# RWKV-7 chunk inverse: first products of one direction share a wave with second products of the other

## What is computed

```python
def step(S, inp):
    r_t, w_t, k_t, v_t, kk_t, a_t = inp
    sa = jnp.einsum("bhvk,bhk->bhv", S, -kk_t)
    S = S * w_t[:, :, None, :] + sa[..., None] * (kk_t * a_t)[:, :, None, :] + v_t[..., None] * k_t[:, :, None, :]
    return S, jnp.einsum("bhvk,bhk->bhv", S, r_t)
```

## Time and profile before

| | |
|---|---|
| median of 3 runs | 2392.87 us (2391.01 to 2393.35) |
| profiled execution | 2385.16 us, its span 2383.5 us |
| TensorE busy over the span | 2128.2 us, 89% |
| VectorE busy | 851.2 us, 36% |
| ScalarE busy | 392.8 us, 16% |
| GpSimd busy | 156.5 us, 7% |
| first products L1199 | 1920 records, 218 ns each in the middle |
| second products L1210, L1212 | 1920 and 1536 records, 218 ns |
| the inverse of the first pair starts at | 611.0 us |
| the last second product of the last pair at | 1204.6 us |

### The profile page before, as it was taken

The page is one execution under the profiler, slowest core; times in us unless marked ns, Lnnn a source line. Parts: engine busy times, 40 slices in busy tenths (PEclk is TensorE's granted clock), DMA queues, the critical chain, the costliest instruction groups (busy, mean ns, idle before and its releaser), DMA issues. The chain is left out here.

```text
span 2383.5 us, 38135 instructions
## 1 busy us (share of the span) xinstructions
PE 2128.2 (89%) x16348; PEld 1071.7 (45%) x16348; DVE 851.2 (36%) x1816; ACT 392.8 (16%) x788; POOL 156.5 (7%) x185
## 2 busy tenths in 40 slices
PE   5787799979999999999979979889988998899886
PEld 2244455535666666665655543224322432243222
DVE  1262243434565666666631032112211221122113
ACT  1111112222322332233101010001000100010002
POOL 0000111110110111011101000000000000000000
PEclk9798899999999999999989989999999999999998
DMA  9932899963121211111113199999999999999996
GB/s 365 354 86 84 279 343 354 336 203 82 50 51 41 51 41 49 41 51 39 47 49 97 53 356 413 413 413 413 413 413 413 413 413 413 413 413 413 413 413 269
DMA packets 271136, 594.01 MB, mean 249 GB/s; under 512 B 25869, under 2 KB 166247, under 8 KB 249863
## 3 DMA queue, kind: packets, MB, share of 16 engines
q1 hardware_dynamic: 253575, 524.64, 59.0%
q0 software_dynamic: 17408, 67.11, 7.4%
HBM read 586.89 MB, written 4.82 MB: 248 GB/s over the span
## 5 line engine op out<-in xcount | busy, mean ns | idle before, releaser
L1852 PE MATMUL bank<-arena,picked 128*64 128x512 f32 x1280 | 301.6, 616 | 50.4 <-DMA arena<-exp_w_up 47.7
L1076 PE MATMUL bank<-arena,w_rkv 128*128 128x384 f32 x768 | 283.7, 504 | 12.7 <-DMA w_rkv<-w_in 8.2
L2031 DVE TENSOR_TENSOR x_sum<-x_sum,bank 128x512 f32<-128x512 f32 x180 | 115.4, 684 | 325.6 <-PE bank L1837 325.6
L1852 PEld LDWEIGHTS bank<-arena,picked 128*64 128x64 f32 x1280 | 97.5, 141 | 245.9 <-issue 245.1
L1076 PEld LDWEIGHTS bank<-arena,w_rkv 128*128 128x128 f32 x768 | 136.9, 190 | 102.7 <-issue 18.6
L1852 PE MATMUL bank<-w_exp,picked 128*64 128x512 f32 x768 | 174.9, 597 | 8.5 <-DMA w_exp<-exp_w_up 8.2
L1876 PE MATMUL bank<-w_exp,hid 128*64 128x512 f32 x768 | 176.4, 598 | 6.7 <-DMA w_exp<-exp_w_down 6.7
L690 PE MATMUL bank<-arena,w_xz 128*128 128x384 f32 x448 | 157.3, 500 | 15.0 <-DMA w_xz<-w_in 15.0
L1918 ACT COPY gu<-bank 112x512 f32<-112x512 f32 x32 | 17.2, 589 | 690.0 <-PE bank L1852 690.0
L690 PEld LDWEIGHTS bank<-arena,w_xz 128*128 128x128 f32 x448 | 82.6, 192 | 94.8 <-issue 30.3
L1049 POOL TENSOR_TENSOR WI<-WX,cst 128x384 f32<-128x384 f32 x80 | 80.9, 1027 | 592.1 <-DVE WX L1505 388.4
(11 more groups left out here) (377 smaller groups left out, 2558.1 us busy)
## 6 DMA issues: line engine op xcount, KB each, us to landing
w_exp<-exp_w_down SPq DMA_DIRECT2D x96, 1024.0 KB, 20.9
arena<-exp_w_gate SPq DMA_DIRECT2D x80, 1024.0 KB, 18.9
arena<-exp_w_up SPq DMA_DIRECT2D x80, 1024.0 KB, 19.0
w_ada<-w_ada POOLq DMA_DIRECT2D x64, 1024.0 KB, 8.2
w_exp<-exp_w_gate SPq DMA_DIRECT2D x48, 1024.0 KB, 18.3
w_exp<-exp_w_up SPq DMA_DIRECT2D x48, 1024.0 KB, 18.5
w_ada<-w_ada SPq DMA_DIRECT2D x32, 1024.0 KB, 17.8
arena<-exp_w_down SPq DMA_DIRECT2D x32, 1024.0 KB, 18.2
```

The lines of the kernel that those rows point to most:

```text
L1076: mm = pe.matmul(ps[feed_bank(i)][:, 0:T], w[:, m % 3, n % 8], hT[:, n % KC], start=(n % KC == 0), stop=(n % KC == KC - 1))
L1852: mm = pe.matmul(ps[b][COLS[j], :], picked[:, k, at:at + 64], halves[j][:, c * 1024 + b * 512:c * 1024 + (b + 1) * 512], start=(k == 0), s ...
L2031: V.tensor_tensor(y, y if e else x, ps[(LAST_BANKS[i // 2 % 4] if e == LAST else 6) + i % 2][:], ALU.add).then_inc(S("added"), 1)
```

## The change

TensorE's ten bursts of each pair become eleven waves. `wave(d, n)` holds the first products of direction d of level n and the second products of the other direction o = 1 - d, of level n - 1 if d is 0, of level n if d is 1. It waits for all of its inputs at its head. Wave (0,1) has only first products, wave (0,6) only second ones of direction 1. Inside a chunk the order is: first product of head 0, XT's product, first product of head 1, XT's product, then the two products for X. Behind each wave stand two or three feed matmuls (38 before the inverse's end, as before), `gate(p)` moves from the end of level 2 to behind wave (0,3), and `front` of TensorE moves to behind waves (0,3), (1,3), (0,4) and (1,4). ScalarE's copies keep their order, with the copy of g and some front steps now between them. On VectorE the updates, `end` and the FRONT steps keep their order; only the adds of output chunks move (table ADDS).

```diff
             AHEAD = (2, 4, 8, 11)
-            per_level = ((0, 2, 0, 4), (0, 2, 0, 4), (0, 2, 0, 3), (0, 2, 0, 2), (0, 4, 0, 2))
-            FED = [AHEAD[3] + sum(sum(per_level, ())[:n]) for n in range(21)]
+            FED = 38
...
-                for n in range(1, 6):
-                    for d in range(2):
+                def wave(d, n):
+
+
+                    o, m = 1 - d, n - 1 + d
+                    firsts, seconds = n <= 5, m >= 1
+                    if firsts:
                         pe.wait_ge(S(f"CT_ready{d}"), 5 * p + n)
                         pe.wait_ge(S(f"X_ready{d}"), 5 * p + n)
-                        hold()
-                        for c in range(NCH):
+                    if seconds:
+                        pe.wait_ge(S(f"P1_out{o}"), 5 * p + m)
+                    hold()
+                    for c in range(NCH):
+                        at = slice(c * Q, (c + 1) * Q)
+                        for h in range(2):
+                            here, there = HP[h], HP[1 - h]
+                            if firsts:
+                                m1 = pe.matmul(ps[3 * d][there, at], CT[d][here, c], X[d][here, c], start=True, stop=True)
+                            if seconds and m < 5:
+                                m2 = pe.matmul(ps[3 * o + 2][there, at], P1[o][there, c], XT[o][there, c], start=True, stop=True)
+                        if seconds:
                             for h in range(2):
...
+                                m2 = pe.matmul(ps[3 * o + 1][HP[h], at], XT[o][HP[1 - h], c], P1[o][HP[1 - h], c], start=True, stop=True)
+                    if firsts:
+                        m1.then_inc(S(f"P1_in{d}"), 1)
+                    if seconds:
+                        m2.then_inc(S(f"D_in{o}"), 1)
...
+                for n in range(1, 6):
+                    wave(0, n)
+                    if n == 3:
+                        more_of(2)
+                        gate(p)
+                        more_of(1)
+                    else:
+                        more_of((3, 3, 0, 2, 2)[n - 1])
+                    if n in (3, 4) and more:
+                        front(p + 1, n - 3 + n // 4)
+                    wave(1, n)
+                    more_of((3, 3, 2, 2, 2)[n - 1])
+                    if n in (3, 4) and more:
+                        front(p + 1, 2 * n - 5)
+                wave(0, 6)
+                more_of(FED - fed)
...
+            ADDS = {(1, 0): 1, (2, 1): 2, (4, 1): 3, (5, 1): 4}
...
-                        if d == 1 and n != 3:
-                            add_part(p, (1, 2, None, 3, 4)[n - 1])
+                        if (n, d) in ADDS:
+                            add_part(p, ADDS[(n, d)])
```

More of the change, by code:

```diff
@@ L1191, in body @@
                 feed(p, AHEAD[3] - 1, AHEAD[3])
-                for n in range(1, 6):
-                    for d in range(2):
+                def wave(d, n):
+                    o, m = 1 - d, n - 1 + d
+                    firsts, seconds = n <= 5, m >= 1
+                    if firsts:
                         pe.wait_ge(S(f"CT_ready{d}"), 5 * p + n)
                         pe.wait_ge(S(f"X_ready{d}"), 5 * p + n)
-                        hold()
-                        for c in range(NCH):
-                            for h in range(2):
[L1199 to L1221, removed]
@@ new lines, in wave, with more_of @@
+                    if firsts:
+                        m1.then_inc(S(f"P1_in{d}"), 1)
+                    if seconds:
+                        m2.then_inc(S(f"D_in{o}"), 1)
+                fed = AHEAD[3]
+                def more_of(k):
+                    nonlocal fed
+                    feed(p, fed, fed + k)
+                    fed += k
+                for n in range(1, 6):
[12 more added lines that the diff above has]
+                        front(p + 1, 2 * n - 5)
@@ L1230, in body @@
                 mm.then_inc(S("PU_in"), 1)
-                feed(p, FED[20], ROUND[0])
+                feed(p, FED, ROUND[0])
                 for d in range(2):
@@ L1347, in body, with P1_copy @@
                     root(p - 1)
+                def P1_copy(d, n):
+                    act.wait_ge(S(f"P1_in{d}"), 5 * p + n + 1)
+                    nc.scalar.copy(P1[d], c6(ps[3 * d][:, 0:T])).then_inc(S(f"P1_out{d}"), 1)
                 for n in range(1, 6):
[L1349 to L1356, removed]
+                    P1_copy(0, n)
+                    if n == 3:
                         if prev:
@@ L1361, in body @@
                         nc.scalar.copy(g[:], ps[7][:, 0:T]).then_inc(S("g_out"), 1)
+                    if n in (3, 4) and more:
+                        front(p + 1, 2 * n - 6)
+                    P1_copy(1, n)
+                    if n in (1, 4) and more == 2:
+                        raw_in(p + 2, n // 4)
                     if n in (3, 4) and more:
```

## The result

The change makes the kernel slower: 2426.44 us (2423.8 to 2427.74) against 2392.26 us (2391.01 to 2393.35) of the kernel before beside it, ratio 1.0142, 95% interval 1.0124 to 1.0159. That is +34 us, where +18 was forecast.

The account below looks back on a forecast made before the run. It took TensorE's instructions plus its few waits to bound the kernel. Pairs 2 to 6 give 9.7 us, pair 1 -0.5, the last two +8.9: +18 us, median 2411 us, range 2401 to 2432.

Parts of the forecast that it names:

- the block: VectorE's end of the previous pair plus this pair's bonus: 5.99 us, from 10.2 to 16.2 us after wave (0,1) starts.
- The mixed wave costs what a burst does: TensorE's mixed waves: 12 products in the fullest quadrant, so 1.55 us each, and the mixing as such gains nothing.
- Rivals 1 and 4: Rival 1: order inside waves costs, 2419, upper end 2461, chance 0.12. Rival 4: first products ride along, 2366, chance 0.06.
- the 0.2 laid out: TensorE, per pair: one more run of fed matmuls together with the half waves costs +0.2 us.
- A new wait of 2.4 us ahead of wave (0,3): TensorE, pairs 2 to 8: subtractions of direction 0 queue behind VectorE's block, wave starts at 17.35 in place of 14.94.
- Rival 3: Ahead of wave (0,3): the stall is covered because VectorE's block ends 2.3 us sooner; 2393, no change; chance 0.10.
- The level-5 wait of 0.8: TensorE in level 5: today's 0.60 us wait and its restart, 0.8 together, would be gone from each pair.
- Adds in the last two pairs: Adds of output chunks wait behind X updates after waves (1,1), (0,3), (0,5): 9.0 us for both pairs, +4.4.
- Three fed with the projection's wait unchanged (0.74 and the restart): TensorE behind wave (1,1): three fed matmuls run from 4.53 to 7.58 us, the projection's wait staying 0.74 us plus restart.
- The pair's sum of +1.94: Per pair: +2.41 new stall, +0.2 extra run and half waves, +0.12 last X, -0.8 level 5.
- The clock stays: TensorE's granted clock was expected to stay at 1.00 throughout the trace of after.
- The rival: Rival 2: the clock falls in the new stall, about 1.5 us seven times, +10, 2421 (twice as long, 2432); chance 0.12.

Follow-up runs that it names:

- the burst kernel: Kernel before, bursts kept, two VectorE front steps and one fed matmul moved later: 2382.35 us; with the last two pairs in old order 2380.6 us.
- e1_split: Changed kernel with VectorE's block cut in two, the later part behind the update of level 2, direction 0, two front steps one place later: 2402.62 us.
- e2_raw: Changed kernel with the fed matmul that begins a projection moved from behind wave (1,1) to behind wave (0,2): 2399.39 us.
- e6_fillraw: Changed kernel with two unused matmuls ahead of the fed matmul that waits for the projection's copy, pairs 1 to 6: 2426.41 us.

## Why the prediction held, and where it was off

The time lies in the stated range of 2401 to 2432 us, and 7 us above the forecast's own range of 2403 to 2419. By its own signs the forecast was wrong in two: the block starts at 11.6 us and not at 10.2, and the clock isn't 1.00 throughout.

- *The mixed wave costs what a burst does.* Right: 1.55 us at full clock, with half waves of 0.85. Rivals 1 and 4 fall by these rows, and the burst kernel shows the waves cost TensorE 0.27 us a pair, near the 0.2 laid out.
- *A new wait of 2.4 us ahead of wave (0,3), because VectorE's block stands there.* Right in size (2.37, pair 2 1.85 with the fed matmuls at the low clock), place and number (seven), and e1_split shows the cause: same work, block cut (two front steps go one update later with it), wait gone. Rival 3 falls. The block's length, which I called soft, was 5.99 us again.
- *The level-5 wait of 0.8 is gone.* It is: no such wait is in the list of after.
- *Adds in the last two pairs: 9.0 us in six places, +4.4.* Right in the sum: 12.8 us in eight places, less the two of 2.02 ahead of an inverse, is 8.8.
- *"Three fed with the projection's wait unchanged (0.74 and the restart)".* This step failed, and no rival had it. I took ScalarE's copy to wait for TensorE's last matmul of the projection; it waits as well for VectorE's first front step, which must have read the buffer that it fills. Before, both were due at the same moment: the last matmul ended at 1010.18, the step at 1010.15, and the copy began at 1010.24. In the wave order the step begins behind wave (1,1) and ends 2.86 us after that wave, while the two matmuls are through after 1.5. The term is 2.07 us where 0.74 stood: +1.33 for each of six pairs, 8 us of the 16 missing. The pair's sum of +1.94 becomes +3.2 with it (81.69 less 78.49 = 3.20), and everything behind stands 1.4 us later than laid out (block at 11.6 us, not 10.2). In the trace of after the copy starts 0.09 us behind the step and 1.4 behind the last matmul (867.67 against 867.58 and 866.28), and e2_raw bears it out.
- *The clock stays.* I gave its fall 0.12, as a price of one wait. It fell, and the forecast lacks it: +1.0 and +1.5 us in pairs 2 and 3, and at 0.50 in pair 7 a stretch of 10.2 us and two of 3.4 (from 1154.2 and 1198.6), in pair 8 one of 3.4 (from 1239.5). These two pairs came out at +12.0 and +6.3, 18.3 where I had 8.9. The rows of both kernels split that: TensorE idles 3.9 and 4.3 us more in them, 8.2 together, and is busy 8.1 and 2.0 us longer with the same work, 10.1, which is the clock but for some 0.3 of waves. The rival named only the wait ahead of wave (0,3), and no low stretch of the changed kernel's two traces begins there. They begin behind the wait for the copy (e6_fillraw shows that the wait ahead of wave (0,3) can do it too) and behind waits of 1.87 to 2.12 us for an add. Why the clock stays down for 10 us in pair 7, and why most waits of this length have no fall behind them, is not shown.
- *The sum.* +18 laid out, and 8.0 (copy) + 2.5 (clock, pairs 2 and 3) + 9.4 (pairs 7 and 8, clock) = 38, against 37.6 in the traces and 34 in the medians. The sign and the forecast wait (16.0 us in the list) were right. That the range held the time is in part luck: rivals had widened it upwards, the copy's 8 us stood in none of them, and the clock fell at other waits than the rival's.

## What to carry to other kernels

When two chains that shared their waits are set half a step apart, go through every other engine's list at its new times: here the waves themselves cost TensorE 0.27 us a pair, and the loss came from two VectorE steps that kept their places while TensorE's cover for them moved, and from the low clock behind the waits that this and the adds made. For a wait that looks settled, look for all its releasers: two that were due within 0.1 us of each other look like one. And try the reordering on the old structure too: with the same kind of moves the old one gains 0.35 to 0.4% too, without the change.

## What the runs showed of the hardware

- One idle time of 2.07 us in a pair is enough for the granted clock to fall to 0.50 (1.2 GHz of 2.4) behind it in every other pair (e1_split). From the first burst of pair 1 to the end of the last inverse the twelve traces have 38 stretches of low clock. Each begins between 0.2 us before and 1.6 us after the end of a TensorE idle time of 1.87 to 2.52 us, and lasts 3.4 us, but for six of 10.2 and one of 6.8. Idle times of this size allow the fall and don't force it: the kernel before has 2.02, 1.82 and 2.02 us (the first stands in the earlier trace rows) and no fall in its trace, and most of the waits of 2.07 and 2.37 us have none either. The Trainium skill, "TensorE: Matmul & The Clock Gate", section "HAM oscillation", ties the fall to idle gaps between bursts; the traces agree in kind. The gaps that it tells of are longer than these, and here the rows decide.
- A wave of 72 records (36 products of 64x64x64) takes 1.55 us at the full clock (863.17 to 864.72) and 2.76 at half (1137.17 to 1139.93 in pair 7).
- The quadrants of the array took f32 products of 64x64x64 side by side at 0.13 us each, 12 in the fullest in 1.55 us, in both orders in which the two kernels ask for them.
- The VectorE scaling L1438 took 1.21 us at 880.62, beside GpSimd's mask from 880.62 to 881.62. Six of its eight times a mask began within 0.01 us of it, and it took 1.20 to 1.21; the other two, and all eight in e1_split, no mask ran beside it, and it took 0.42. That agrees with the exclusive lock of a port pair in the Trainium skill, "SBUF — State Buffer", section "SBUF: two separate sides": the scaling ended 0.21 us behind the mask.
